# A decoder layer on one core: the state-space stage with tokens in partitions, the dt chain between the projections, and the last stage inside the expert block

## What is computed

```python
dt = softplus(dt_raw + dt_bias);  a = -exp(a_log)
xd = x * dt[..., None];  da = dt * a            # in chunks of 128 tokens
da_cs = cumsum(da)                              # within the chunk
decay_in = exp(segsum(da))                      # exp(cs[l] - cs[s]) for s <= l
cb = einsum("bclgn,bcsgn->bcgls", cm, bm)
y_diag = einsum("bcgls,bgrcls,bcsgrp->bclgrp", cb, decay_in, xd)
states = einsum("bclgn,bgrcl,bclgrp->bcgrpn", bm, exp(da_cs[..., -1:] - da_cs), xd)
h = h * exp(da_cs[..., -1]) + states            # from chunk to chunk; prev is h before
y_off = einsum("bclgn,bcgrpn,bgrcl->bclgrp", cm, prev, exp(da_cs))
y = (y_diag + y_off + d_skip * x) * silu(z)
y = y * rsqrt(mean(y * y over each group) + EPS) * norm_w
...
out = rms_norm(x1 + g2 * routed_experts(h2)) * final_norm_w
```

## Time and profile before

| | |
|---|---|
| median of 3 runs | 3237.61 us (3229.97 to 3243.84) |
| the profiled execution | 3242.88 us, span 3241.3 us |
| mean granted TensorE clock | 0.933 of full |
| busy: TensorE, VectorE, ScalarE, GpSimd | 2826.8, 2441.5, 1524.0, 544.3 us |
| HBM read, written | 733.62 MB, 82.84 MB |

### The profile page before, as it was taken

How to read it: one execution, slowest core, us unless ns; L and a number is a source line. 1 busy time by engine, 2 the same in 40 slices (tenths; PEclk the granted TensorE clock), 3 DMA queues, 4 the chain that set the end, 5 groups by cost and what they waited for, 6 DMA issues and landing times. The chain is left out here.

```text
span 3241.3 us, 36581 instructions
## 1 busy us (share of the span) xinstructions
PE 2826.8 (87%) x12749; PEld 2291.0 (71%) x12749; DVE 2441.5 (75%) x1854; ACT 1524.0 (47%) x1254; POOL 544.3 (17%) x432
## 2 busy tenths in 40 slices
PE   2799999999996759899883999999999999999970
PEld 2677777777864647677673788788877888788850
DVE  5878888777537985676745888888888888888859
ACT  5322222222113321000021888888887888888842
POOL 0000000000004545455400111111111111111100
PEclk7899999999997889999965999999999999999985
DMA  9711121216412107777653899999889999899968
GB/s 329 251 52 58 58 65 58 65 59 209 136 52 65 49 29 232 234 236 242 216 217 119 326 357 365 369 390 373 351 348 365 396 393 360 352 377 381 382 241 368
DMA packets 252518, 771.98 MB, mean 238 GB/s; under 512 B 25176, under 2 KB 119432, under 8 KB 183612
## 3 DMA queue, kind: packets, MB, share of 16 engines
q1 hardware_dynamic: 189714, 613.76, 50.1%
q10 hardware_dynamic: 50810, 115.73, 10.3%
q0 software_dynamic: 11952, 41.97, 3.2%
HBM read 733.62 MB, written 82.84 MB: 252 GB/s over the span
## 5 line engine op out<-in xcount | busy, mean ns | idle before, releaser
L1933 DVE TENSOR_TENSOR wlo<-wraw,whi 128x2048 fp32r<-128x2048 f32 x444 | 1006.3, 2288 | 181.8 <-ACT whi L1882 181.7
L1882 ACT ACTIVATE whi<-wraw 128x2048 fp32r<-128x2048 f32 x444 | 843.7, 1916 | 243.9 <-PE ps L1867 115.2
L1813 PE MATMUL ps<-whi,xhi 128*128 128x512 f32 x1184 | 474.9, 401 | 0.4 <-DVE wlo L1933 0.4
L1815 PE MATMUL ps<-whi,xlo 128*128 128x512 f32 x1184 | 462.9, 391 | 0.0
L1814 PE MATMUL ps<-wlo,xhi 128*128 128x512 f32 x1184 | 462.0, 390 | 0.0
L347 PE MATMUL ps<-hh,wih 128*128 128x512 f32 x1056 | 335.4, 398 | 2.4 <-DVE wil L335 2.4
L347 PE MATMUL ps<-hl,wih 128*128 128x512 f32 x1056 | 329.4, 393 | 0.0
L347 PE MATMUL ps<-hh,wil 128*128 128x512 f32 x1056 | 329.3, 393 | 0.0
L678 DVE SCALAR_TENSOR_TENSOR acc<-u,vcur,acc 128x1024 f32<-128x1024 f32 x240 | 308.3, 1284 | 7.7
L1815 PEld LDWEIGHTS ps<-whi,xlo 128*128 128x128 f32 x1184 | 222.7, 188 | 47.5
L1813 PEld LDWEIGHTS ps<-whi,xhi 128*128 128x128 f32 x1184 | 224.0, 189 | 42.1 <-issue 0.8
(11 more groups left out here) (332 smaller groups left out, 4527.2 us busy)
## 6 DMA issues: line engine op xcount, KB each, us to landing
wraw<-in_w_gate_dram SPq DMA_DIRECT2D x148, 1024.0 KB, 8.7
wraw<-in_w_up_dram SPq DMA_DIRECT2D x148, 1024.0 KB, 7.1
wraw<-in_w_down_dram SPq DMA_DIRECT2D x148, 1024.0 KB, 7.6
slot<-in_w_mod_dram ACTq DMA_DIRECT2D x96, 512.0 KB, 4.7
wraw_i<-in_w_in_dram SPq DMA_DIRECT2D x72, 512.0 KB, 3.9
wmA<-in_w_mod_dram SPq DMA_DIRECT2D x54, 512.0 KB, 5.4
wraw_o<-in_w_out_dram SPq DMA_DIRECT2D x64, 256.0 KB, 4.3
y<-ybuf_d SPq DMA_DIRECT2D x16, 1024.0 KB, 12.6
```

Source lines behind the costliest of these rows:

```text
L1813: pe.matmul(dst, xhi[:, t, :], whi[:, s, w], start=(t == 0), stop=False)
L1815: last = pe.matmul(dst, xlo[:, t, :], whi[:, s, w], start=False, stop=(t == KT - 1))
L1882: act.activation(whi[:, spl(m), :], wraw[:, raw(m), :], ACT.Copy).then_inc(s_whi, 1)
L1933: dve.tensor_tensor(wlo[:, spl(m), :], wraw[:, raw(m), :], whi[:, spl(m), :].bitcast(F32), ALU.subtract).then_inc(s_wsp[raw(m)], 1)
```

## The change

*Block 1.* TensorE's dt projection now stands before the seventh SSD tile, its transposes before the ninth, and before the last one three new products (`da_sums`): the running sums with tokens in partitions, the chunk totals, and the running sums with heads in partitions. The small operations stand at the same places of ScalarE's and VectorE's orders (tiles 7 to 9), and the rounding of dt's weights moves from GpSimd to ScalarE and VectorE. The weights lie in `sq`, so modulation rows are loaded in three slots where there were four. Behind the last tile:

```diff
+def dt_columns():
+    pe.wait_ge(s_dtc, 1)
+    for j in range(TT):
+        last = pe.transpose(ps[:, 3584 + j * H:3584 + (j + 1) * H], sq[0:H, j * P:(j + 1) * P], ident[0:H, 0:H])
...
+def da_sums():
+    pe.wait_ge(s_da, 1)
+    rhs = da[:].rearrange("p j h -> p (j h)")
+    pe.matmul(ps[:, 3072:3200], tri[:], rhs, start=True, stop=True)
+    pe.matmul(ps[:, 3200:3328], ones[:], rhs, start=True, stop=True)
+    pe.matmul(ps[:, 3328:3456], rhs, tri[:], start=True, stop=True).then_inc(s_cs0, 1)
+for n in range(3, XT):
+    if n == 6:
+        dt_proj()
+    if n == 8:
+        dt_columns()
+    if n == 11:
+        da_sums()
+    pe.wait_ge(s_pad, n - 2)
+    proj(pe, n % 3, n // 3 + NA)
```

```diff
+def cs_copies():
+    dve.wait_ge(s_cs0, 1)
+    flat = lambda a: a.rearrange("p j h -> p (j h)")
+    dve.tensor_copy(flat(dx[5]), ps[:, 3328:3456]).then_inc(s_csr, 1)
+    dve.tensor_copy(flat(dx[6]), ps[:, 3072:3200]).then_inc(s_csr, 1)
+    dve.tensor_copy(flat(dx[0]), ps[:, 3200:3328]).then_inc(s_csr, 1)
+    dve.wait_ge(s_csr, 3)
+    dve.tensor_tensor(dx[1], dx[0], dx[6], ALU.subtract).then_inc(s_dcs, 1)
```

```diff
+act.wait_ge(s_csr, 3)
+act.dma_start(cst_d[:, :], dx[5].rearrange("p j h -> p (j h)")).then_inc(s_cst, 16)
+act.activation(dx[7], dx[6], ACT.Exp).then_inc(s_cse, 1)
+act.wait_ge(s_dcs, 1)
+act.activation(dx[1], dx[1], ACT.Exp).then_inc(s_cse, 1)
+act.activation(dx[0], dx[0], ACT.Exp).then_inc(s_cse, 1)
+for s, n in ((s_zs, NA), (s_ys, NA), (s_ms, 2), (s_xs, XT), (s_cst, 1)):
```

*Block 2.* The sums, their exponentials and dt times the decay stay in `dd` from block 1 for all chunks. The running sums are stored in `cst_d`, one row of 128 tokens for each head and chunk, and SyncE loads a chunk's 16 rows into all partitions (`csb`); ScalarE makes the decay with one Relu for each head and two exponentials. Loads run three chunks deep for `xc` and `zc`, two for `csb`:

```diff
+def load(j):
+    b = j % 3
+    if j >= 3:
+        sp.wait_ge(s_yo, j - 2)
+    cols = slice(j * P, (j + 1) * P)
     sp.dma_start(xc[:, b, :, :], xbc_d[:, :, cols].rearrange("a p n -> p a n")).then_inc(s_ch[b], 16)
+    if j >= 2:
+        sp.wait_ge(s_rel, 2 * j - 2)
+    sp.dma_start(csb[:, j % 2, :, :].rearrange("p h l -> p (h l)"),
+                 cst_d[H * j:H * j + H, :].rearrange("(a h) l -> a (h l)", a=1).broadcast_to((P, H * P))
+                 ).then_inc(s_csb[j % 2], 16)
     sp.dma_start(zc[:, b, :, :], zs_d[:, :, cols].rearrange("a p n -> p a n")).then_inc(s_ch[b], 16)
```

```diff
+def pe_cb(pe, j):
+    pe.wait_ge(s_ch[j % 3], 32 * (j // 3) + 32)
     pe.wait_ge(s_cbm, j)
     for g in range(2):
...
+def pe_x(pe, j):
+    pe.wait_ge(s_hst, j + 1)
+    for q in range(CT):
+        last = pe.transpose(ps[:, BANK_X + q * P:BANK_X + (q + 1) * P], xc[:, j % 3, q, :], ident[:])
+    last.then_inc(s_xt, 1)
...
+def pe_diag(pe, j):
+    if j == 0:
+        pe.wait_ge(s_dg, CT)
+    pe.wait_ge(s_xd, j + 1)
+    pe.wait_ge(s_d, j)
     for g in range(2):
+        pe.wait_ge(s_m, 2 * j + g + 1)
+        for q in range(4 * g, 4 * g + 4):
+            at = BANK_Y + q * P
+            pe.matmul(ps[:, at:at + P], xc[:, j % 3, q, :], diagd[:, q, :], start=True, stop=False)
+            for r in range(2):
+                pe.matmul(ps[:, at + r * HD:at + (r + 1) * HD], ee[:, j % 3, 2 * q + r, :], xd[:, 2 * q + r, :],
+                          start=False, stop=(r == 1))
...
+def pe_off(pe, j):
+    pe.wait_ge(s_hst, j + 1)
+    pe.wait_ge(s_a, j)
     for g in range(2):
+        last = pe.matmul(ps[:, BANK_O + 512 * g:BANK_O + 512 * g + 512], xc[:, j % 3, 10 + g, :],
+                         hst[:, 8 * g:8 * g + 8, :].rearrange("p h d -> p (h d)"), start=True, stop=True)
+    last.then_inc(s_yo, 1)
...
+def pe_states(pe, j):
     pe.wait_ge(s_xdd, j + 1)
     pe.wait_ge(s_bt, j + 1)
+    pe.wait_ge(s_zc, j + 1)
     for g in range(2):
+        last = pe.matmul(ps[:, BANK_X + 512 * g:BANK_X + 512 * g + 512], btok[:, j % 2, g, :],
+                         xdd[:, 8 * g:8 * g + 8, :].rearrange("p h d -> p (h d)"), start=True, stop=True)
+    last.then_inc(s_st, 1)
...
+    pe_cb(pe, 0)
+    pe_x(pe, 0)
+    pe_cb(pe, 1)
+    pe_z(pe, 0)
+    for j in range(TT):
+        pe_diag(pe, j)
+        pe_off(pe, j)
+        if j > 0:
+            pe_y(pe, j - 1, 0)
+        pe_states(pe, j)
+        if j + 2 < TT:
+            pe_cb(pe, j + 2)
+        if j + 1 < TT:
+            pe_x(pe, j + 1)
+        if j > 0:
+            pe_y(pe, j - 1, 1)
+        if j + 1 < TT:
+            pe_z(pe, j + 1)
+    for g in range(2):
+        pe_y(pe, TT - 1, g)
```

ScalarE:

```diff
+    def decay(j, g):
+        if g == 0:
+            act.wait_ge(s_csb[j % 2], 16 * (j // 2) + 16)
+            if j >= 3:
+                act.wait_ge(s_yo, j - 2)
+        for h in range(8 * g, 8 * g + 8):
+            ins = act.activation(ee[:, j % 3, h, :], csb[:, j % 2, h, :], ACT.Relu, scale=-1.0,
+                                 bias=css[:, j, h:h + 1])
+        ins.then_inc(s_rel, 1)
+        act.wait_ge(s_rel, 2 * j + g + 1)
+        e = ee[:, j % 3, 8 * g:8 * g + 8, :].rearrange("p h l -> p (h l)")
+        act.activation(e, e, ACT.Exp, scale=-1.0).then_inc(s_ee, 1)
...
+    for j in range(TT):
+        if j > 0:
+            round_y(j - 1, 0)
+        if j + 2 < TT:
+            copy_b(j + 2)
+        if j + 3 < TT:
+            decay(j + 3, 0)
+        if j > 0:
+            round_y(j - 1, 1)
+        squares(j)
+        if j + 1 < TT:
+            copy_z(j + 1)
+        if j + 3 < TT:
+            decay(j + 3, 1)
```

VectorE (`per_head` spreads one value over a head's 64 columns, `x_dt` and `x_dt_decay` multiply x from PSUM, `lower` makes the low part of y):

```diff
+    def mask(j):
+        dve.wait_ge(s_cb, j + 1)
+        dve.wait_ge(s_bt, j + 1)
+        dve.wait_ge(s_m, 2 * j)
+        dve.tensor_tensor(cbm[:], ps[:, BANK_C:BANK_C + 2 * P].rearrange("p (g l) -> p g l", g=2),
                           tri[:, None, :].broadcast_to((P, 2, P)), ALU.mult).then_inc(s_cbm, 1)
...
+    for j in range(TT):
+        y = yt[:, j % 2, :]
+        dve.wait_ge(s_yo, j + 1)
+        dve.tensor_tensor(heads(y), heads(ps[:, BANK_O:BANK_O + DS]), per_head(ecs, j), ALU.mult).then_inc(s_a, 1)
+        if j + 1 < TT:
+            dve.wait_ge(s_hst, j + 1)
+            dve.tensor_tensor(hst[:], hst[:], per_head(elast, j), ALU.mult).then_inc(s_b, 1)
+            dve.wait_ge(s_st, j + 1)
+            dve.wait_ge(s_b, j + 1)
+            dve.tensor_tensor(hst[:], hst[:], heads(ps[:, BANK_X:BANK_X + DS]), ALU.add).then_inc(s_hst, 1)
+        dve.wait_ge(s_a, j + 1)
+        dve.tensor_tensor(y, y, ps[:, BANK_Y:BANK_Y + DS], ALU.add).then_inc(s_d, 1)
+        if j + 1 < TT:
+            x_dt(j + 1)
+        dve.wait_ge(s_d, j + 1)
+        dve.wait_ge(s_zc, j + 1)
+        dve.tensor_tensor(y, y, zt[:, j % 2, :], ALU.mult).then_inc(s_yz, 1)
+        if j > 0:
+            lower(j - 1, 0)
+        if j + 1 < TT:
+            dve.wait_ge(s_st, j + 1)
+            x_dt_decay(j + 1)
+        if j + 2 < TT:
+            mask(j + 2)
+        if j > 0:
+            lower(j - 1, 1)
...
+            cols = slice(512 * g, 512 * g + 512)
+            dve.scalar_tensor_tensor(out=yn[:, j % 2, cols], in0=yt[:, j % 2, cols], scalar=yrs[:, j, g:g + 1],
+                                     in1=snrow[:, cols], op0=ALU.mult, op1=ALU.mult).then_inc(s_yn, 1)
```

```diff
+for j in range(TT):
+    if j >= 2:
+        m = FREED[j - 2]
+        sp.wait_ge(s_wsp[raw(m)], raw_turn(n, m) + 1)
+    sp.dma_start(x1_tile(j), x1_d[j * P:(j + 1) * P, :]).then_inc(s_xf[j], 16)
+sp.wait_ge(s_os, 16 * n + 16)
+for j in range(TT):
+    b = j % 3
+    if j >= 3:
+        sp.wait_ge(s_sum3, j - 2)
+    sp.dma_start(y1[:, b, :], ybuf_d[j * P:(j + 1) * P, :]).then_inc(s_y1[b], 16)
+    sp.dma_start(y2[:, b, :], ybuf_d[SEQ + j * P:SEQ + (j + 1) * P, :]).then_inc(s_y1[b], 16)
...
+for j in range(TT):
+    act.wait_ge(s_sum3, j + 1)
+    if j >= 1:
+        act.wait_ge(s_sq3, j)
+    act.activation(junk3[:], x1_tile(j), ACT.Square, accum_out=ssq3[:, j:j + 1]).then_inc(s_sq3, 1)
+    act.wait_ge(s_sq3, j + 1)
+    act.activation(rst3[:, j:j + 1], ssq3[:, j:j + 1], ACT.Sqrt, bias=epsc[:], scale=1.0 / D).then_inc(s_std3, 1)
+    if j >= 1:
+        act.wait_ge(s_of3, j)
```

More of the change, by code:

```diff
@@ L922, in toks @@
-            def toks(a, j):
-                return a[:, :, ds(j * P, P)] if not isinstance(j, int) else a[:, :, j * P:(j + 1) * P]
-            def half(a, g):
-                return a[:, 8 * g:8 * g + 8, :]
+            zt = sb(st, "zt", [P, 2, DS])
+            yt = sb(st, "yt", [P, 2, DS])
+            yn = sb(st, "yn", [P, 2, DS])
+            snrow = sb(st, "snrow", [P, DS])
+            diagd = sb(st, "diagd", [P, CT, P])
+            ysj = sb(st, "ysj", [P, 2, 512])
+            yssq = sb(st, "yssq", [P, TT, 2])
@@ new lines, in pe_cb, with pe_z @@
+                    last.then_inc(s_cb, 1)
+                def pe_x(pe, j):
[3 more added lines that the diff above has]
+                    last.then_inc(s_xt, 1)
+                def pe_z(pe, j):
+                    pe.wait_ge(s_xdd, j + 1)
+                    for q in range(CT):
+                        last = pe.transpose(ps[:, BANK_X + q * P:BANK_X + (q + 1) * P], zc[:, j % 3, q, :], ident[:])
+                    last.then_inc(s_zt, 1)
@@ new lines, in round_y @@
+                    def round_y(j, g):
+                        act.wait_ge(s_ytr, 2 * j + g + 1)
+                        act.activation(toks(ysh, g, j), tiles(ps[:, BANK_T:BANK_T + 512]), ACT.Copy).then_inc(s_hi, 1)
```

(11 more changed lines are left out.)

544 lines of the change are left out of this document (197 added, 347 removed).

## The result

The change makes the kernel faster: 3192.5 us, the median of 4 runs (3187.2 to 3197.1), against 3240.7 before (4 runs, 3230.0 to 3246.6), a ratio of 0.985 with a 95% interval of 0.982 to 0.989, or 48 us. The forecast was 3176, its range 3152 to 3202. The profiled execution took 3187.2 us, its span is 3185.6, which is 55.7 us less than the 3241.3 before.

A forecast was written before the change was run, and what follows sets the result against it. VectorE was taken to bound the state-space stage, with many passes, partly stretched by GpSimd. Gains of 56.7 us there and 5.0 in the last stage, 61.7 off the 3237.6 median, gave 3176 us; range 3152 to 3202.

The forecast's parts named there:

- The 64-column matmuls: State-space chunk, 16 new TensorE products: 0.223 us each, as for 128 columns; lower end 0.14.
- the clock's term: State-space chunk: 1.6 us added for TensorE running partly below full clock; 11.3 if at the lower level throughout.
- The ring: State-space chunk: chain between TensorE and VectorE from one state's addition to the next, 17.4 us; 19.0 with the clock.
- the lower level lasts: Rival: idle stretches keep TensorE at 1.2 GHz, a chunk takes 28.7 us, total 3242, no change; chance 0.04.
- The start: Projections' end to the state-space stage: with the dt projection moved, the stage starts at 982.0, costing 3.9 us.
- that cover: Projections: fewer load slots and two moved conversions hide under each tile's 22 us projection; uncovered, under 2 us.
- First state: State-space stage's beginning: loading two chunks and computing until the first state is ready, 33 us, bounds 25 and 39.
- Tail: State-space stage's last chunk, which hands on no state: 25 us to the stage's end.
- Last stage: After the last scatter: y's reload waits for the landing, not the block's end; gain 5.0 us, bounds 1.0 and 6.6.
- ScalarE's second ring: Rival: in the state-space chunks, ScalarE's chain behind the broadcast rows sets the pace, 22.3 us a chunk, 3196; chance 0.13.
- The faster ring: Rival: weights don't pace the 64-column products and the clock stays high, 16.1 us a chunk, 3159; chance 0.12.
- Broadcast rows at a trickle: Rival: few DMA engines serve the state-space row loads, 57 us instead of 7.1, a chunk 43 us, 3320; chance 0.02.

The follow-up runs named there:

- experiments 1 and 2: Kernel before with four GpSimd products narrowed: stage 199.3 us, 3281.0 us with more experts' work; changed kernel with 110 added GpSimd products: stage 188.3, 3193.2 us.
- experiment 5: Changed kernel with the eight D times x products moved from the diagonal part to behind the x transposes: 3158.3 us, 0.976 of before.
- Experiment 4: Changed kernel with the exponential of a_log moved from ahead of the first SSD tile's Silu to dt's first exponential: 3178.8 us, one run.
- experiment 8: Changed kernel with a block's end put back between the expert block and the last stage's sums: 3194.7 us, one run.
- (7): Changed kernel with four more ScalarE copies of 512 columns in each chunk, ahead of the squares: 3185.1 us, one run.

## Why the prediction was right

*The stage, what bounded it.* Right, and confirmed from both sides: passes long beside GpSimd's work (experiments 1 and 2) and the chain behind them. What the text called stretching is waiting for the end of GpSimd's instruction, and the reciprocal, named among the long passes, takes its 1.75 us without GpSimd too. The new passes take 1.2 and 0.7 us, as priced.

*The 64-column matmuls.* Right: 0.223 us was taken against 0.14. Eight groups of one 128-column and two 64-column matmuls go from 1070.80 to 1076.27, 0.228 a matmul, and 0.221 in experiment 5 where they are 64-column ones alone. At the lower level eight groups take 10.1 us (1027.0 to 1037.1), 0.42 a matmul: the diagonal part doubles, as the clock's term had it.

*The ring.* Right. It was put at 17.4 us at full level, and the chunks at a clock of 0.91 take 18.2, the 0.8 more being the z transposes at the lower level (1.8 us instead of 0.9). The sum had 19.0 with 1.6 for the clock; the mean of six is 19.7. The five later ones take 18.9 on average. The first takes 23.9, 4.9 more than forecast, since its diagonal and state parts ran at 0.50 throughout: the rival "the lower level lasts" came true in one chunk of six. The term for the clock was sized as a mean of 1.6 us; over the 17.4, chunks took 0.8, 1.9 and, the first, 6.5 us. That their mean, 2.3, lies near 1.6 is partly luck, since nothing in the forecast said how many chunks would be like the first.

*The start.* The step that failed: "If that cover went, it would be under 2 us." The small operations at the beginning of the SSD tiles weren't covered. The exponential of a_log, moved ahead of the first Silu, brings two table loads, which made TensorE wait 2.7 us longer and then run at the lower clock for part of 10 us. Experiment 4 takes 4.7 us back, of the 5.7 by which the stage's start was missed (982.0 forecast, 987.7 measured). A table load had its price in rows 5, but the forecast costed this exponential nowhere: it had stood where nothing waited, after the last tile's Silu.

*First state.* 33 us forecast, 32.9 measured, and that so close is luck. The z transposes ended 19.6 us after the first load (19 forecast), the diagonal and state parts took 8.2 (10), and VectorE 5.0 to the addition's end (4): a product with the mask, which had waited for ScalarE's decays, stood ahead of its scale. ScalarE's decays were not on the forecast's path.

*Tail.* 25 us forecast from the last addition, 28.0 measured (1138.8 to 1166.8). 0.9 of it is the ring's part up to the state part (14.5 against 13.6), and 1.9 are the last chunk's squares, which stand in ScalarE's order behind the rounding of the second half of chunk 6, and this behind TensorE's transposes:

```profile
1158.47 0.60 ACT L1131 ACTIVATE ysh<-ps 128x512 fp32r<-128x512 f32 x1 [4.12 <-PE ps L1064]
1158.96 0.62 ACT L1124 ACTIVATE ysj<-yt 128x512 f32<-128x512 f32 x1
```

The gate had ended at 1157.05. The sum took the squares as following the gate.

*Last stage.* 5.0 us taken, 6.6 measured, the upper end; experiment 8 shows 6.5 for the block's end alone. Choosing the row at hand in full would have been right.

*The sum.* Start 5.7 later, first ring 4.9, tail 3.0, less 0.2 and 0.6 elsewhere: the stage ended 12.8 us later than forecast (1166.8 for 1154.0). The gain was to be 61.7; stage and last block gave 50.6, and the medians 48. That the time is 16 us above the forecast and not 11 is within what medians of 3 and 4 runs vary by.

*The rivals.* ScalarE's second ring: not closed (7). The faster ring of 16.1 us: its condition, 64-column matmuls of 0.14 us, didn't hold; 15.5 us came about another way, with the D x products elsewhere (5). Broadcast rows at a trickle: the rows land in 7.5 us. The dt chain gains nothing: it was worth 2.9 us, though the stage starts later than before all the same, for the new sums and the a_log exponential.
